# Expert weights through a ring of eight 2 MB slots in order of use, with loops over four experts, in a hybrid decoder block

## The chip, the cores and the metric

One Trainium2 chip, one core of it. The metric is the device time of one execution in microseconds; the kernel before was run three times and its median stands for it.

## What is computed

A decoder block for 512 tokens of width 1024, all in float32: RMS norm, an input projection, two attention mixers (NSA with compressed, selected and window keys; FoX with forget gates), gated output projections, a residual sum x2, and a mixture of 32 experts, four for each token. The part the change touches is the mixture:

```
logits = xt @ router_w + router_b;  top_v, top_i = top_k(logits, 4);  gate = softmax(top_v)
# for each expert e, over the tokens routed to it
hc  = xb @ w1[e] + b1[e]                      # (tokens, 1024) @ (1024, 2048)
gt  = minimum(hc[:, :1024], 7);  up = clip(hc[:, 1024:], -7, 7)
y   = ((up + 1) * gt * sigmoid(1.702 * gt)) @ w2[e] + b2[e]     # @ (1024, 1024)
out = x2 + sum of gate * y;  then a final RMS norm
```

An expert's weights are 8 MB (w1) and 4 MB (w2); all 32 have to be read once, 402 MB.

## The kernel before

The program is written engine by engine, with semaphores. The attention part takes the time to about 445 us, the output projection and the routing the time to about 536 us. PE then runs expert after expert: `expert(e, b, before)` (L1652) runs `up` (L1614), the product with w1 for 96 token slots in three groups of 32, and then `second(e - 1, ...)` (L1675) with `down` (L1628), the product with w2 for the expert before. `up` reads w1 in eight slabs of 1 MB, `down` reads w2 in four. Each matmul works on 32 columns of the array (`tile_position`), four beside each other. Expert 0 to 2 and 31 are written out; experts 3 to 30 stand in a hardware loop whose body has two of them (L1692):

```python
            with pe.Fori(0, (E - 4) // 2) as i:
                expert(2 * i + 3, 1, True)
                expert(2 * i + 4, 0, True)
```

The weights lie in `ring` (L162), twelve slabs of 1 MB, loaded in pairs of 2 MB by `load_pair` (L619) on the queue of SyncE (SP). The slots are tied to a place in an expert: pairs 0 to 3 hold w1, pairs 4 and 5 hold w2. SP waits until PE has used a pair (`w1_used`, `w2_used`) and loads the same pair of a later expert; the order of its loads is w1 of expert e + 1, then w2 of expert e (L667). Before the experts `ring` holds attention weights, so w1 of expert 0 is loaded as these come free, from 441 us on, and w2 of expert 0 behind the first gather.

Around the start of expert 0 SP also stores the normalized rows (`store_table`, L631) and the residual rows `xs` (`store_x2`, L635) to DRAM. The last table store must land before GpSimd (POOL) may gather expert 0's rows from the table (L831), PE turns them (`turned_x`), VectorE (DVE) scales them (L2158), and expert 0 begins. Routing: DVE writes one-hot rows in `qk` (`mark`, L2053); PE's `fill_table` makes the table of slots from them, and `fill_gates` (L1536), 33 small matmuls behind expert 0's `up`, the gates' part for the last tile, which DVE takes up in `take_gates` (L2084).

`up` writes PSUM banks 0 to 2 for every expert, the bias bank is 3, `down` writes 4 and 5. DVE reads banks 0 to 2 in `biased` (L2180) and then gives them back with `hc_free` (L2202); PE waits for it before the next `up` (L1657). ScalarE (ACT) copies the bias bank (`take_b_up`, L1140), takes the sigmoid, and scales `down`'s result by the gate (`take_y`); POOL adds it to x2 in DRAM by indirect DMA (`scattered`, L853).

Behind the experts every engine passes a loop for overflow blocks (L1701), whose body is jumped over when an expert has no more than 96 tokens; 21 rounds. Then x2 is read back, normalized with the gain `gf_b` and stored.

## Time and profile before

| | us |
|---|---|
| three runs | 1585.99, 1589.96, 1591.88 (median 1589.96) |
| profiled execution, its own time | 1584.68 |
| its span | 1582.9 |
| PE matmuls busy | 1534.0 (97%) |
| weight loads (PEld) busy | 849.8 (54%) |
| VectorE, GpSimd, ScalarE busy | 510.6, 312.5, 247.4 |
| granted PE clock, mean | 0.99 |
| DMA | 468 MB, 296 GB/s over the span |

The profile covers one execution. Each engine has a line of busy time; PE's weight loads overlap its matmuls. "PEq" or "PEldq" is PE's sequencer, which runs branches and register instructions, SPq is the queue of DMA issues. The chain of waits follows what released each step back from the last instruction.

### The profile page before, as it was taken

The numbers are of one execution on the slowest core, as the hardware profiler recorded it, in microseconds if no ns is written. First come the engines' busy times: TensorE is split into PE (matmuls) and PEld (weight loads), VectorE is DVE, ScalarE is ACT, GpSimd is POOL, SyncE is SP. The second block draws the span as 40 slices with busy tenths as digits, with TensorE's granted clock in tenths as the row PEclk, the third lists the DMA queues.
The fourth block names the chain that finished last, engine by engine and source line by source line (L and its number), as shares of the span: only waits on it lengthen the run. The fifth ranks groups of instructions, "written<-read, shape, count | busy, mean of one in ns | idle before, by whom it ended". The sixth has DMA issues, their size and how long they took to land.

```text
span 1582.9 us, 31267 instructions
## 1 busy us (share of the span) xinstructions
PE 1534.0 (97%) x13039; PEld 849.8 (54%) x13040; DVE 510.6 (32%) x941; ACT 247.4 (16%) x509; POOL 312.5 (20%) x449
## 2 busy tenths in 40 slices
PE   7999999999999999999999999999999999999993
PEld 4655555665445533566666666666664334555331
DVE  4104555242425542233223322332232223322232
ACT  4213443232422100000000000010001000000001
POOL 2000002342200202122212121222122212121101
PEclk9999999999999999999999999999999999999997
DMA  8121131521261599999999999999999999999986
GB/s 237 27 66 42 40 80 27 170 80 30 66 263 53 214 397 407 406 414 414 413 407 415 415 410 409 414 415 410 409 417 414 409 409 416 414 415 408 413 350 216
DMA packets 108446, 468.17 MB, mean 296 GB/s; under 512 B 29591, under 2 KB 71615, under 8 KB 83794
## 3 DMA queue, kind: packets, MB, share of 16 engines
q1 hardware_dynamic: 94610, 446.55, 70.1%
q0 software_dynamic: 13792, 21.00, 6.0%
q8 instruction: 31, 0.51, 0.1%
q14 instruction: 13, 0.11, 0.0%
HBM read 452.41 MB, written 19.29 MB: 298 GB/s over the span
## 4 chain that ended last, share of the span: by engine, by line
PE 78%; DMA 17%; DVE 2%; issue 1%; ACT 1%; SPq 0%; DVEq 0%; PEld 0%; POOL 0%; ACTq 0%; PEldq 0%; POOLq 0%
PE ps L1624 33%; DMA ring<-in_expert_w 16%; PE ps L1220 12%; PE ps L1642 10%; PE ps L1367 7%; PE ps L1646 5%; PE ps L1556 4%; PE ps L1352 2%; PE ps L1329 2%; PE ps L1339 1%; ACT mixT L1023 1%; DMA ring<-x 0%; DMA xs<-in_x 0%; PE ps L1508 0%; PE ps L1532 0%
## 5 line engine op out<-in xcount | busy, mean ns | idle before, releaser
L1624 PE MATMUL ps<-ring,oT_fox 128*32 128x512 f32 x6144 | 671.4, 592 | 2.8 <-DMA ring<-in_expert_w 2.8
L1624 PEld LDWEIGHTS ps<-ring,oT_fox 128*32 128x32 f32 x6144 | 333.5, 110 | 317.0 <-issue 278.9
L1642 PE MATMUL ps<-ring,hT 128*32 128x512 f32 x2048 | 292.7, 592 | 0.9 <-DMA ring<-in_expert_w 0.9
L2182 DVE TENSOR_TENSOR mixT<-ps,mask 128x768 f32<-128x768 f32 x64 | 61.0, 953 | 680.1 <-PE ps L1624 680.1
L1646 PE MATMUL ps<-ring,hT 128*32 128x256 f32 x2048 | 186.1, 379 | 0.0
L1646 PEld LDWEIGHTS ps<-ring,hT 128*32 128x32 f32 x2048 | 110.3, 110 | 106.1 <-issue 103.0
L1367 PE MATMUL ps<-hT,ring 128*128 128x512 f32 x304 | 137.0, 597 | 0.0
L1147 ACT ACTIVATE mixT<-mixT 128x768 f32<-128x768 f32 x32 | 27.0, 845 | 616.3 <-DVE mixT L2186 616.3
L1642 PEld LDWEIGHTS ps<-ring,hT 128*32 128x32 f32 x2048 | 100.3, 110 | 22.0 <-DMA ring<-in_expert_w 1.8
L843 POOL DMA_INDIRECT oT_nsa<-table,pc x93 | 100.6, 1082 | 47.4 <-POOL pc L838 28.0
L1220 PE MATMUL ps<-hT,ring 128*128 128x512 f32 x208 | 90.4, 593 | 0.2 <-ACT hT L953 0.2
L838 POOL COPY pc<-pc 128x3 int32 (+1 forms) x31 | 5.9, 191 | 427.3 <-DMA x<-hT,v_win 395.0
L1367 PEld LDWEIGHTS ps<-hT,ring 128*128 128x128 f32 x304 | 55.4, 190 | 63.7 <-issue 63.7
L1157 ACT ACTIVATE hT<-ps,v_fox 128x512 f32<-128x512 f32 x64 | 33.7, 577 | 270.3 <-PE ps L1646 270.3
L863 POOL COPY pT<-pT 96x32 bf16 (+1 forms) x64 | 15.4, 242 | 253.7 <-ACT hT L1157 239.8
L1220 PEld LDWEIGHTS ps<-hT,ring 128*128 128x128 f32 x208 | 39.1, 190 | 47.9 <-issue 47.7
L1023 ACT ACTIVATE mixT<-ps,st 128x128 f32<-128x128 f32 (+1 forms) x96 | 49.1, 536 | 78.8 <-DVE st L1855 78.8
L1556 PE MATMUL ps<-ring,mixT 128*128 128x512 f32 x128 | 59.0, 601 | 2.1 <-DVE qk L1986 2.1
L854 POOL DMA_INDIRECT x<-hT,v_win x32 | 52.1, 1629 | 39.4 <-POOL v_win L851 24.5
L2171 DVE STREAM_TRANSPOSE oT_fox<-oT_nsa 128x768 f32<-128x768 f32 x31 | 49.6, 1601 | 13.3 <-DVE mixT L2190 6.8
L856 POOL DMA_INDIRECT x<-hT,v_win x32 | 50.5, 1579 | 9.8 <-issue 9.8
L2178 DVE STREAM_TRANSPOSE hT<-mixT 128x768 f32<-128x768 f32 x32 | 51.3, 1604 | 1.1
(303 smaller groups left out, 1148.7 us busy)
## 6 DMA issues: line engine op xcount, KB each, us to landing
ring<-in_expert_w SPq DMA_DIRECT2D x192, 2048.0 KB
ring<-in_w_in SPq DMA_DIRECT2D x28, 512.0 KB, 5.0
ring<-in_w_out SPq DMA_DIRECT2D x8, 512.0 KB, 8.7
ring<-in_w_in SPq DMA_DIRECT2D x1, 2144.0 KB, 12.8
xs<-in_x SPq DMA_DIRECT2D x4, 512.0 KB, 5.2
ring<-in_w_in SPq DMA_DIRECT2D x8, 256.0 KB, 3.6
ring<-in_w_proj_nsa SPq DMA_DIRECT2D x16, 128.0 KB, 2.8
ring<-in_w_proj_fox SPq DMA_DIRECT2D x8, 256.0 KB, 3.2
```

The costliest lines, as they stand in the source:

```text
L843: pool.indirect_dma_start(out=xg_rows[b][:, 256 * g:256 * g + 256], out_offset=None, in_=table_quarter, in_offset=bass.IndirectOffsetOnAxi ...
L854: pool.indirect_dma_start(out=x2_half, out_offset=bass.IndirectOffsetOnAxis(ap=now_half[b], axis=0), in_=yb[b][:, 0:512], in_offset=None, ...
L856: pool.indirect_dma_start(out=x2_quarter, out_offset=bass.IndirectOffsetOnAxis(ap=now_quarter[b], axis=0), in_=yb[b][:, 512:768], in_offse ...
L1023: last = act.activation(probs[:, h, P_OFF[t]:P_OFF[t] + P * (t + 1)], scores(h, t), ACT.Exp, bias=ngm[:, h, t:t + 1], accum_out=sums[:, h, ...
L1220: last = pe.matmul(dst, lhs(c), rhs(c), start=(c == 0), stop=(c == n - 1))
L1367: ins = pe.matmul(w, w_c(c), hT[:, c, :], start=(c == 0), stop=(c == NK - 1))
L1556: ins = pe.matmul(ps[:, u, :], mixT[:, k, t * P:(t + 1) * P], w_o[k][:, n * 512:(n + 1) * 512], start=(k == 0), stop=(k == NK - 1))
L1624: ins = pe.matmul(wide(ps[TG * j:TG * j + TG, g, :]), xT[b][:, g, c, :], up_slab(c, j), start=(c == 0), stop=(c == NK - 1), tile_position= ...
L1642: pe.matmul(ps[TG * q:TG * q + TG, 4, :], gT[b][:, q // 2, c, :], ring[:, NK + j, at:at + 512], start=False, stop=(c == NK - 1), tile_posi ...
L1646: ins = pe.matmul(ps[TG * q:TG * q + TG, 5, 0:256], gT[b][:, 2, c, :], ring[:, NK + j, at:at + 256], start=False, stop=(c == NK - 1), tile ...
L2178: return dve.transpose(gT[b], act_b.rearrange("p g (m c) -> p g c m", c=NK))
L2182: return dve.tensor_tensor(to, half, b_up[:, 256 * n:256 * n + 256].unsqueeze(1).broadcast_to([P, NG, 256]), ALU.add)
```

## The change

Two more slots join the ring, so that it has eight of 2 MB. Slot 6 is `xs`, the residual rows, free when the last of them is stored. Slot 7 is a new tensor `x0` of 4096 columns, which holds what were `qk` (one-hot rows and attention queries), `rope_cos`, `rope_sin`, `pcT` and `cmp_one`; it is free when `fill_gates` has read the one-hot rows.

The loads go through the slots in the order in which PE uses them: w1 of expert 0, w1 of expert 1, w2 of expert 0, w1 of expert 2, w2 of expert 1, and so on, load number n into slot n mod 8, once load n - 8 has been used. Six loads an expert and eight slots come round after four experts, so the loops of SP and PE have bodies of four experts and seven passes instead of 14 for PE.

Expert 0's `up` writes banks 5 to 7 and the gates' late part bank 2, so that expert 1 need not wait for `hc_free`. `fill_gates` moves to behind the third slab of expert 0, `take_gates` on VectorE ahead of the rows of expert 1, and expert 1 waits for `rows_ready` at its start. ACT's copy of the bias of expert 1 now waits for `hc_free`. The final gain goes to `xs` only when all of w2 has been used.

```diff
+SLOTS = 8
...
-        qk = sb("qk", [P, 4, S])
+        x0 = sb("x0", [P, 4096])
+        qk = x0[:, 0:4 * S].rearrange("p (a s) -> p a s", a=4)
...
-        pcT = sb("pcT", [P, S])
+        pcT = x0[:, 6 * S:7 * S]
...
-        cmp_one = sb("cmp_one", [P, NT, 2, NCP])
-        rope_cos = sb("rope_cos", [P, S])
-        rope_sin = sb("rope_sin", [P, S])
+        cmp_one = x0[:, 7 * S:7 * S + NT * 2 * NCP].rearrange("p (t h c) -> p t h c", t=NT, h=2)
+        rope_cos, rope_sin = (x0[:, n * S:(n + 1) * S] for n in (4, 5))
...
-        hc_g, hc_u = ps[:, 0:NG, 0:256], ps[:, 0:NG, 256:512]
+        HC, HC_FIRST = 0, BANKS - NG
+        hc_g, hc_u = ([ps[:, at:at + NG, 256 * n:256 * n + 256] for at in (HC, HC_FIRST)] for n in range(2))
...
-            return ps[0:CAP, 5, 3 * e:3 * end].rearrange("p (e v) -> p e v", v=3)
+            return ps[0:CAP, 2, 3 * e:3 * end].rearrange("p (e v) -> p e v", v=3)
...
+        def pair_slot(k):
+            if k < 6:
+                return ring[:, 2 * k:2 * k + 2, :].rearrange("p c n -> p (c n)")
+            return xs_f if k == 6 else x0[:, :]
+        def slab(k, h):
+            return pair_slot(k)[:, 2048 * h:2048 * h + 2048]
+        def up_slab(k, h, j):
+            return slab(k, h).rearrange("p (n j m) -> p n j m", n=2, j=4)[:, :, j, :]
+        class Order:
+            def __init__(self, i, r):
+                self.i, self.r = i, r
+            def w1(self, u):
+                return Fill(self.i, 6 * self.r - 2 + u if self.r else u)
+            def w2(self, u):
+                return Fill(self.i, 6 * self.r + 8 + u if self.r < E - 1 else 6 * self.r + 4 + u)
+        class Fill:
+            def __init__(self, i, at):
+                self.slot, self.landed = at % SLOTS, 48 * i + 16 * (at // SLOTS + 1)
...
-            load_pair(0, 0)
+            load_w1_pair(0, 0, 0)
             sp.wait_ge(mix_sig, NK)
             for u in range(1, 3):
-                load_pair(0, u)
+                load_w1_pair(0, u, u)
             sp.wait_ge(mix_full, NK)
-            load_pair(0, 3)
+            load_w1_pair(0, 3, 3)
             for t in range(NT - 1):
                 store_x2(t)
                 store_table(t)
             sp.wait_ge(out_full, 2 * NT)
+            load_w1_pair(1, 0, 4)
             store_table(NT - 1)
             sp.wait_ge(xg_loaded[0], 16)
             store_x2(NT - 1)
-            for u in range(NK // 2, 6):
-                load_pair(0, u)
-            def load_w1(e):
-                for u in range(NK // 2):
-                    sp.wait_ge(w1_used, NK * (e - 1) + 2 * u + 2)
-                    load_pair(e, u)
-            def load_w2(e):
+            load_w1_pair(1, 1, 5)
+            sp.wait_ge(x2_stored, 16 * (NT + 1))
+            load_w1_pair(1, 2, 6)
+            sp.wait_ge(table_full, NT + 3)
+            load_w1_pair(1, 3, 7)
+            def load_w2(e, order):
                 for u in range(2):
-                    sp.wait_ge(w2_used, 4 * (e - 1) + 2 * u + 2)
-                    load_pair(e, NK // 2 + u)
-            load_w1(1)
-            with sp.Fori(1, E - 1) as e:
-                load_w1(e + 1)
-                load_w2(e)
-            load_w2(E - 1)
-            sp.wait_ge(x2_stored, 16 * (NT + 1))
+                    if order.r == E - 1:
+                        sp.wait_ge(w2_used, 4 * (e - 2) + 2 * u + 2)
+                    elif isinstance(e, int) and e == 0:
+                        sp.wait_ge(w1_used, 2 * u + 2)
+                    else:
+                        sp.wait_ge(w1_used, NK * e + 2 * (u + 2) + 2)
+                    load_w2_pair(e, u, order.w2(u).slot)
+            def load_w1(e, order):
+                for u in range(4):
+                    if u >= 2:
+                        sp.wait_ge(w1_used, NK * (e - 1) + 2 * (u - 2) + 2)
+                    elif isinstance(e, int) and e == 2:
+                        sp.wait_ge(w1_used, 2 * (u + 2) + 2)
+                    else:
+                        sp.wait_ge(w2_used, 4 * (e - 3) + 2 * u + 2)
+                    load_w1_pair(e, u, order.w1(u).slot)
+            load_w2(0, Order(0, 0))
+            load_w1(2, Order(0, 2))
+            load_w2(1, Order(0, 1))
+            with sp.Fori(0, (E - 4) // 4) as i:
+                for r in range(3, 7):
+                    load_w1(4 * i + r, Order(i, r))
+                    load_w2(4 * i + r - 1, Order(i, r - 1))
+            load_w1(E - 1, Order(0, E - 1))
+            load_w2(E - 2, Order(0, E - 2))
+            load_w2(E - 1, Order(0, E - 1))
+            sp.wait_ge(w2_used, 4 * E)
...
                 act.wait_ge(w1_used, NK * e + 1)
+                if isinstance(e, int) and e == 1:
+                    act.wait_ge(hc_free, 1)
                 act.activation(b_up, ps[:, NG, :], ACT.Copy).then_inc(b_up_ready, 1)
...
-            def expert(e, b, before):
+            def expert(e, b, before, order):
+                fills = [order.w1(u) for u in range(4)]
                 pe.wait_ge(xT_ready, e + 2)
-                if before:
+                if isinstance(e, int) and e == 1:
+                    pe.wait_ge(b_up_ready, 1)
+                    pe.wait_ge(rows_ready, 1)
+                elif before:
                     pe.wait_ge(hc_free, e)
                 pe.wait_ge(pick_up_ready, e + 1)
@@ -1660,19 +1716,28 @@
                     ins.then_inc(w1_used, 1)
                     if isinstance(e, int) and e == 0 and c == 0:
                         spread_slots()
+                    if isinstance(e, int) and e == 0 and c == 2:
+                        fill_gates()
                     if isinstance(e, int) and e == 1 and c == NK // 2:
-                        pe.wait_ge(rows_ready, 1)
                         spread_rows(4, 0, 2 * E, row_of.rearrange("p v e -> p (v e)")).then_inc(table_full, 1)
                 if not before:
                     pe.wait_ge(parts_taken, 1)
-                up(b, lambda c: pe.wait_ge(slabs_loaded[c // 2], 16 * e + 16) if c % 2 == 0 else None, used)
+                def loaded(c):
+                    if c % 2 == 0:
+                        pe.wait_ge(slabs_loaded[fills[c // 2].slot], fills[c // 2].landed)
+                up(b, [f.slot for f in fills], loaded, used, HC if before else HC_FIRST)
                 if before:
-                    second(e - 1, 1 - b)
-                else:
-                    fill_gates()
-            def second(e, b):
+                    second(e - 1, 1 - b, Order(order.i, order.r - 1))
...
             keep_clock(2)
-            expert(0, 0, False)
-            expert(1, 1, True)
-            expert(2, 0, True)
-            with pe.Fori(0, (E - 4) // 2) as i:
-                expert(2 * i + 3, 1, True)
-                expert(2 * i + 4, 0, True)
-            expert(E - 1, 1, True)
-            second(E - 1, 1)
+            for e in range(3):
+                expert(e, e % 2, e > 0, Order(0, e))
+            with pe.Fori(0, (E - 4) // 4) as i:
+                for r in range(3, 7):
+                    expert(4 * i + r, r % 2, True, Order(i, r))
+            expert(E - 1, 1, True, Order(0, E - 1))
+            second(E - 1, 1, Order(0, E - 1))
...
             count_extra()
+            take_gates()
             take_x(1, 1, gather)
             expert(0, 0, None)
-            take_gates()
             after_first()
             with dve.Fori(0, E // 2 - 1) as i:
```

`load_w1_pair` and `load_w2_pair` do what `load_pair` did, with the slot given; in `down` the operand `ring[:, NK + j, ...]` becomes `slab(slots[j // 2], j % 2)`.

Two places in the engines' order show the moves. SP, from the last residual and table stores to its expert loop; first before, then with the change (`x<-in_expert_w` is the slot in `x0`, `xs<-in_expert_w` the one in `xs`):

```order
L633 DMA table<-hT 128x1024 [waits x_normed]
L633 DMA table<-hT 128x1024 [waits x_normed,out_full]
L637 DMA x<-xs 128x1024 [waits x2_ready,xg_loaded0]
L628 DMA ring<-in_expert_w 128x4096 x2
L628 DMA ring<-in_expert_w 128x4096 [waits w1_used] x4
L667 UNCONDITIONAL_BRANCH
L667 ISA
```

```order
L664 DMA table<-hT 128x1024 [waits x_normed]
L654 DMA ring<-in_expert_w 128x4096 [waits out_full]
L664 DMA table<-hT 128x1024 [waits x_normed]
L668 DMA x<-xs 128x1024 [waits x2_ready,xg_loaded0]
L654 DMA ring<-in_expert_w 128x4096
L654 DMA xs<-in_expert_w 128x4096 [waits x2_stored]
L654 DMA x<-in_expert_w 128x4096 [waits table_full]
L660 DMA ring<-in_expert_w 128x4096 [waits w1_used] x2
L654 DMA ring<-in_expert_w 128x4096 [waits w1_used] x4
L660 DMA xs<-in_expert_w 128x4096 [waits w1_used]
L660 DMA x<-in_expert_w 128x4096 [waits w1_used]
L714 UNCONDITIONAL_BRANCH
L714 ISA
```

A load of expert 1 now stands ahead of the last table store and three behind the last residual store, where two loads of w2 of expert 0 stood. Those now follow the whole of expert 1's w1.

PE from the second half of expert 0's `up` to the first matmuls of expert 1; before, then with the change:

```order
L1624 MATMUL ps<-ring,oT_fox 32x512 [waits slabs_loaded2]
L1624 MATMUL ps<-ring,oT_fox 32x512 x23
L1624 MATMUL ps<-ring,oT_fox 32x512 [waits slabs_loaded3]
L1624 MATMUL ps<-ring,oT_fox 32x512 x23
L1538 MATMUL ps<-kT_win,qk 96x96 [waits gates_ready]
L1541 MATMUL ps<-v_sel,qk 96x3 x32
L1618 MATMUL ps<-pT 32x512 [waits pick_up_ready,hc_free,xT_ready]
```

```order
L1674 MATMUL ps<-ring,oT_fox 32x512 x11
L1588 MATMUL ps<-kT_win,x 96x96 [waits gates_ready]
L1591 MATMUL ps<-v_sel,x 96x3 x32
L1674 MATMUL ps<-ring,oT_fox 32x512 x12
L1674 MATMUL ps<-ring,oT_fox 32x512 [waits slabs_loaded2]
L1674 MATMUL ps<-ring,oT_fox 32x512 x23
L1674 MATMUL ps<-ring,oT_fox 32x512 [waits slabs_loaded3]
L1674 MATMUL ps<-ring,oT_fox 32x512 x23
L1668 MATMUL ps<-pT 32x512 [waits rows_ready,pick_up_ready,b_up_ready,xT_ready]
```

The two rows of the gate matmuls moved up into expert 0, and the first matmul of expert 1 waits for `b_up_ready` and `rows_ready` where it waited for `hc_free`.

## Rows read from the trace of the kernel before

**Rows 1.** The page: busy time of each engine, and busy tenths in 40 slices.

```profile
PE 1534.0 (97%) x13039; PEld 849.8 (54%) x13040; DVE 510.6 (32%) x941; ACT 247.4 (16%) x509; POOL 312.5 (20%) x449
...
DMA  8121131521261599999999999999999999999986
```

**Rows 2.** Stretches: us, busy (x) PE, PEld, DVE, ACT, POOL, PEclk, DMA share, GB/s.

```profile
656.20:750.60 94.40, 94.40 (x1001) 60.14 (x996) 26.83 (x27) 7.54 (x13) 21.69 (x30) 1.00 1.02 412
...
1405.60:1470.20 64.60, 64.13 (x676) 33.11 (x668) 17.90 (x19) 4.99 (x8) 15.33 (x21) 1.00 1.02 413
```

**Rows 3.** The chain of waits in order of time: start us, us, what.

```profile
593.15 20.60 PE ps L1624 x144
...
1191.22 20.79 PE ps L1624 x185
...
1212.17 26.50 DMA ring<-in_expert_w
...
1238.71 5.40 PE ps L1624 x48
...
1470.21 26.48 DMA ring<-in_expert_w
...
1512.96 20.60 PE ps L1624 x192
...
1543.78 0.48 PE ps L1646 x8
...
1557.13 0.48 PE ps L1646 x8
```

**Rows 4.** Timeline of PE: start us, us, engine, line; in expert 22, and at the end.

```profile
1222.65 15.63 PE L1624 MATMUL ps<-ring,oT_fox 128*32 128x512 f32 x144
...
1533.38 0.40 PE L1631 MATMUL ps<-pT 96*32 96x512 bf16 x4
...
1545.43 0.40 PE L1631 MATMUL ps<-pT 96*32 96x512 bf16 x4 [1.22 <-issue]
```

**Rows 5.** Timeline before the first gather; GB/s in 521 to 536 us; gather to landing.

```profile
520.37 1.10 PE L1556 MATMUL ps<-ring,mixT 128*128 128x512 f32 x2
...
526.15 0.32 SPq L633 DMA_DIRECT2D table<-hT  x1
...
534.91 12.99 SPq L628 DMA_DIRECT2D ring<-in_expert_w  x4
...
GB/s 0 0 0 0 0 0 0 0 0 0 0 0 0 0 0 76 382 404 437 98 0 0 0 0 0 0 0 0 44 98 98 251 273 109 22 0 0 0 317 393
...
DMA to landing us min/median/max: 4.7/4.7/4.7
```

**Rows 6.** Timeline, PE and VectorE where expert 1 begins.

```profile
557.73 0.24 PE L1538 MATMUL ps<-kT_win,qk 128*96 128x96 f16 x1
...
561.05 0.40 PE L1618 MATMUL ps<-pT 96*32 96x512 bf16 x4 [1.68 <-issue]
...
552.68 1.59 DVE L2171 STREAM_TRANSPOSE oT_fox<-oT_nsa 128x768 f32<-128x768 f32 x1 [6.44 <-DMA oT_nsa<-table,pc]
```

**Rows 7.** DMA in 593 to 691 us, then 700 to 1500: packets, MB, share.

```profile
DMA packets 3904, 40.05 MB, mean 409 GB/s; under 512 B 600, under 2 KB 988, under 8 KB 1584
...
q8 instruction: 8, 0.13, 0.5%
...
DMA packets 32483, 329.76 MB, mean 412 GB/s; under 512 B 5191, under 2 KB 8547, under 8 KB 13366
...
oT_nsa<-table,pc POOLq DMA_INDIRECT x75, 7.6
```

**Rows 8.** The branch of the expert loop, and the weight load behind it.

```profile
L1692 PEldq COMPARE_BRANCH  x14: 76/208/208, 685.6 to 1511.0; - x14
...
686.94 0.24 PEld L1618 LDWEIGHTS ps<-pT 96*32 96x32 bf16 x4
```

**Rows 9.** The branch over the overflow body: min/median/max ns.

```profile
L1702 PEldq COMPARE_BRANCH  x21: 214/214/3357, 1559.9 to 1578.1; - x21
```

More of the change, by code:

```diff
@@ L460, in hybrid_block @@
         idx_ready = sem("idx_ready")
-        slabs_loaded = [sem("slabs_loaded%d" % b) for b in range(6)]
+        slabs_loaded = [sem("slabs_loaded%d" % b) for b in range(SLOTS)]
         w1_used = sem("w1_used")
@@ L1612, in wide, with up @@
                 return c.rearrange("p (n m) -> p n m", n=2)
-            def up(b, loaded, used):
+            def up(b, slots, loaded, used, hc=HC):
                 for j in range(4):
@@ L1623, in up, with down @@
                         for j in range(4):
-                            ins = pe.matmul(wide(ps[TG * j:TG * j + TG, g, :]), xT[b][:, g, c, :], up_slab(c, j),
+                            ins = pe.matmul(wide(ps[TG * j:TG * j + TG, hc + g, :]), xT[b][:, g, c, :],
+                                            up_slab(slots[c // 2], c % 2, j),
                                             start=(c == 0), stop=(c == NK - 1), tile_position=(0, TG * j))
                     used(c, ins)
-            def down(b, loaded, used):
+            def down(b, slots, loaded, used):
                 for q in range(4):
@@ L1637, in down @@
                     j, h = c // 2, c % 2
+                    rows = slab(slots[j // 2], j % 2)
                     if h == 0:
@@ L1668, in expert, with second, loaded @@
                     pe.wait_ge(parts_taken, 1)
-                up(b, lambda c: pe.wait_ge(slabs_loaded[c // 2], 16 * e + 16) if c % 2 == 0 else None, used)
+                def loaded(c):
+                    if c % 2 == 0:
+                        pe.wait_ge(slabs_loaded[fills[c // 2].slot], fills[c // 2].landed)
+                up(b, [f.slot for f in fills], loaded, used, HC if before else HC_FIRST)
                 if before:
-                    second(e - 1, 1 - b)
-                else:
-                    fill_gates()
-            def second(e, b):
+                    second(e - 1, 1 - b, Order(order.i, order.r - 1))
+            def second(e, b, order):
+                fills = [order.w2(u) for u in range(2)]
+                def loaded(j):
+                    if j % 2 == 0:
+                        pe.wait_ge(slabs_loaded[fills[j // 2].slot], fills[j // 2].landed)
                 pe.wait_ge(gT_ready, e + 1)
@@ L1682, in second @@
                 pe.wait_ge(pick_down_ready, e + 1)
-                down(b, lambda s: pe.wait_ge(slabs_loaded[(NK + s) // 2], 16 * e + 16) if s % 2 == 0 else None,
-                     lambda s, ins: ins.then_inc(w2_used, 1))
+                down(b, [f.slot for f in fills], loaded, lambda j, ins: ins.then_inc(w2_used, 1))
             pe.wait_ge(count_taken, 1)
@@ L1716, in _ @@
                     pe.wait_ge(ov_w, 192 * o + 192)
[L1717 removed]
+                    up(0, range(4), lambda c: None, lambda c, ins: ins.then_inc(ov_pe, 1) if c == NK - 1 else None)
                     pe.wait_ge(ov_dve, 3 * o + 3)
[L1719 removed]
+                    down(0, (4, 5), lambda s: None, lambda s, ins: ins.then_inc(ov_pe, 1) if s == 3 else None)
                     pe.wait_ge(ov_act, 2 * o + 4)
@@ L2260, in _ @@
                     dve.wait_ge(b_up_ready, E + o + 1)
-                    for n, (to, half) in enumerate(((gt_b, hc_g), (up_b, hc_u))):
+                    for n, (to, half) in enumerate(((gt_b, hc_g[0]), (up_b, hc_u[0]))):
                         biased(to, half, n).then_inc(ov_part, 1)
```

31 lines of the change are left out of this document (14 added, 17 removed).

## The prediction

> **What bounds the kernel now.** I read the page first. TensorE (PE) is busy for 97% of the span and the DMA slices stand at 9 from the middle of the run on [rows 1]: from about 535 us, where the experts begin, two resources are both nearly full. The table of stretches shows how they share the time. In 656 to 751 us PE is busy for 94.40 of 94.40 us while DMA moves 412 GB/s; in 1406 to 1470 us DMA moves 413 GB/s, no more, and PE is short of work for about half a microsecond [rows 2]. So DMA runs at its own pace in both stretches, and PE is a little faster than it.
>
> The chain of waits gives both paces. From the up projection that starts at 593.15 to the one at 1191.22 there are 19 experts: 598.07 / 19 = 31.48 us each, PE alone. From 1212.17 to 1470.21 the chain is a weight load and one pair of slabs, eight times: 258.04 / 8 = 32.26 us for an expert's six loads, 5.38 us a load, DMA alone [rows 3]. The loads lose 0.78 us an expert against PE until their lead is gone, at 1238.66. What that costs: 1512.96 - 593.15 = 919.8 us for 29 experts, against 29 x 31.48 = 912.9, so 6.9 us. At the end the last expert's w2 pairs may be loaded only when expert 30 has used the two slots. PE starts that last down projection at 1545.43 and ends it at 1557.13 + 0.48 = 1557.6, which is 12.2 us; the one before it went from 1533.38 to 1544.26, 10.9 us. That is 1.3 us more. Both together, **8.2 us**, are all that waiting for weights costs [rows 3, 4].
>
> **The change, part by part.** I follow PE's end, 1557.6 us in this trace. What comes behind it (gates, scatter-add, final norm, store) takes the last 25.3 us of the span of 1582.9 and stays. The norm's gain is now loaded only behind PE's last use of w2; it is needed in the final norm, when the scatter-add has landed and x2 has been read back, so I put it at nothing; without that cover it would be a 0.5 MB transfer, 1.3 us at 412 GB/s.
>
> (a) *Table store before the first gather.* One 2 MB load is now issued when the last output matmul is done, at about 521.5, before the table store of 526.15. The store's bytes move from 526.9 to about 528.3, and the gather waits for them [rows 5]. The load's bytes need 5.1 us at 412 GB/s from about 0.8 us behind its issue, so until 527.4: the store begins some 0.5 us later. I take **+0.5 us** (0 to +1.5) for the start of the first expert.
>
> (b) *First boundary.* Today PE runs the 33 small gate matmuls at 557.73 and then stands for 1.68 us, because expert 1 writes the same PSUM banks and waits until VectorE has read expert 0's [rows 6]. With other banks this wait goes; the gate matmuls merely move into expert 0. Late next would be expert 1's rows: VectorE transposes them at 552.68 for 1.6 us [rows 6] and scales them in about one; the gate work moved ahead of that, five small operations behind gate matmuls that end at about 547, fits into the 6.44 us that it stood for the gather. PE wants the rows at 559.5. So **-1.6 us** (-1.7 to 0).
>
> (c) *Order and number of slots.* The queue of loads starts again at 534.9 in both kernels, but four loads are behind it today and five in the new one; the seventh and the eighth slot are filled at about 538 and 547, while the queue is busy, so they add no gap. Every load thus lands one load earlier in the order of use, 5.4 us. In order of use the last w2 pairs wait for expert 29's slots and not for expert 30's. How far this reaches: w1 pair 3 of expert 22 lands at 1238.66; moved by 5.4 us it lands at 1233.3, where PE, which wants it at 1222.65 + 3 x 5.15 = 1238.1 today [rows 4] and 1.1 us earlier by (a) and (b), wants it at 1237.0: a lead of 3.7 us. It shrinks by 9 x 0.78 = 7.0 us until expert 31, which would wait 3.3 us. If PE is late for another reason by more than that, all 8.2 us of weight waits go: **-8.2 us** then, -4.9 us otherwise.
>
> (d) *The loop over four experts.* PE executes 1001 + 996 matmuls and weight loads in three experts [rows 2], 666 an expert: the loop's body grows from some 1,330 to some 2,660 instructions. In 593 to 691 us, with the first pass of the present loop, the instruction queue brings 8 packets, 0.13 MB; in 700 to 1500 us there is no row of it at all [rows 7]. So the present body stays with the engine once fetched (8 packets for 98 / 31.48 x 666 = 2,070 instructions, one per 259), and its backward branch takes 208 ns, hidden: it is executed 1.4 us before PE needs the next expert's first weights [rows 8]. What a branch costs whose target is not held stands in one row: the first jump over the overflow body, about one expert's instructions ahead, took 3357 ns, the 20 behind it 214 [rows 9]. Will the new body still be held? The only far jump in the trace paid at about 700 instructions, and blocks arrive just ahead of need, none in advance; I take it that a body twice as long is not held, and that each of the six backward branches (seven passes) pays that way. That is a choice: no row shows a backward jump over more than 1,330 instructions.
>
> The Trainium skill, "Runtime: NRT & Kernel Launch", section "Instruction fetch mechanics", says that PE has 128 KiB for 2,048 instructions, refilled in blocks of 256 as a FIFO, and that a taken branch to something outside its window must fetch first. By that rule the new body does not fit. The trace agrees with the block (259 by the rows) and with the stall (3.36 us); the same page's two-block window is at odds with a body of five blocks that runs without a fetch, so for that the trace decides.
>
> The price on PE's path: the branch starts at 685.6; 3.36 us later it ends at 688.9, 0.45 us of register instructions follow, and the first weights go in at 689.4 where today it is 686.94: 2.4 us. That row was taken with DMA nearly idle. Under full load a gather takes 7.6 us to land against 4.7 when idle [rows 5, 7], 1.6 times: 3.15 x 1.6 = 5.1 us instead of 3.15, so 4.4 us on PE's path. The low end, with the register instructions hidden as well, is 2.0. I take **3.3 us**, in the middle, since the load is full but an instruction packet is one piece of 16 KB and a gather is many: 6 x 3.3 = **+19.8 us** (+12 to +26.4). PE never waits for anything else in the loop, so nothing absorbs it; the loads only gain more lead by it.
>
> The sum: +0.5 - 1.6 - 8.2 + 19.8 = **+10.5 us**. The profiled execution took 1584.68 us, so 1595.2 by it; the median of the three runs is 1589.96, 5.3 us above, so **1600.5 us** against that median.
>
> **The rivals.** *Rival 1: the longer body is held* (or a backward branch is foreseen). For it: 1,330 instructions are held today and nothing shows the limit. Against it: the 3357 ns row. Then PE is tied to the loads again from about expert 27 on: 0.5 - 1.6 - 4.9 = -6.0 us, 1584.0 us, between -9.3 (loads a little faster, no wait left) and -3. The point that decides: the branch must cost PE less than (8.2 + 1.1) / 6 = 1.6 us, a little less with the 3.3 us wait counted; then the kernel is faster.
>
> *Rival 2: the instruction packets slow the weights.* If the body is fetched anew in every pass, 8 packets in 98 us are 0.5% of 16 engines, 0.98 us a packet [rows 7]. On one engine alone that is 2.6 us an expert, and as a load lands only when its slowest engine is done, 28 experts would run at up to 34.9 us instead of 32.26: the stream would end 73 us later, and the time be near 1657 us. Against it: in just that stretch DMA moved 409 GB/s against 412 without the packets [rows 7] and the experts stayed at PE's 31.5 us. I give it little.
>
> **How the numbers follow.** A measurement of this kernel tells about 0.5%, 8 us, from no change. Forecast (all six branches pay): 0.70; its own range is +2.7 to +17, 1592 to 1607, with up to 3 us more if a second block is late behind the first. Of it 0.48 lies over +8 us, 0.22 within. Rival 1: 0.25, of which 0.09 beyond -8 and 0.16 within. Rival 2: 0.03, slower. Left over 0.02, half slower, half faster. Slower 0.52, same 0.38, faster 0.10. The range of 8 in 10 takes in most of rival 1 and the costly end of the branches: 1581 to 1610.
>
> **What would show it.** The new loop's COMPARE_BRANCH on PE's sequencer: seven, six of them over 3 us where the old took 0.21, each followed by a pause on PE of 2 to 4.5 us, every fourth expert and 126 to 130 us apart. Instruction packets (16 KB) in the middle of the run, some 2.6 an expert. No wait for in_expert_w on PE anywhere behind expert 2. The pause of 1.68 us at the first boundary gone. The first gather up to 1 us later. A branch of 0.2 us with the instruction queue silent would make the prediction wrong, and rival 1 right; a branch of 3.4 us or more with experts further apart than 31.5 us between the branches would speak for rival 2.

## The result, and the profile after

The changed kernel takes **1625.63 us** (median of 6 runs, 1623.51 to 1626.20), the kernel before on the same chip 1590.48: a ratio of **1.0224, interval 1.0207 to 1.0241**. That is 35 us slower, where the prediction had 10.5 us and a range up to 1610. The profiled execution took 1625.79 us, its span is 1624.0, so 41.1 us more than the span of before. (The profiled execution of before, 1584.68, lies nearly 6 us under its median, so the spans differ by more than the medians.)

The page of the changed kernel, its busy times, the granted clock, the instruction queue and the chain that ended last:

```profile
PE 1543.3 (95%) x13039; PEld 645.7 (40%) x13040; DVE 511.4 (31%) x941; ACT 247.6 (15%) x509; POOL 317.8 (20%) x449
...
DMA  8121130611342899999999999999999999999954
...
q8 instruction: 114, 1.87, 0.5%
...
PE 92%; issue 3%; DVE 1%; ACT 1%; DMA 1%; SPq 0%; DVEq 0%; PEld 0%; POOL 0%; PEldq 0%; POOLq 0%; ACTq 0%
```

Against [rows 1] the matmuls are as many and PE is busy for 9.3 us more with them, in a span 41 us longer. The instruction queue carries 114 packets, where before it had 31. DMA, which held 15.6% of the chain of before by its waits for weights alone, has 1% left; in its place stands "issue".

All that PE waited for from expert 1 to the last, in the view of waits (engine, line, releaser: us in total, times, longest):

```profile
PE ps L1668 <- issue: 32.6, 6, 5.7
PE ps L1682 <- issue: 1.2, 1, 1.2
```

No weight is waited for any more; six waits for "issue" stand ahead of L1668, the first matmul of an expert. What PE's sequencer did there, as in [rows 8], and the jump over the overflow body, as in [rows 9] (min/median/max ns):

```profile
L1755 PEldq COMPARE_BRANCH  x7: 76/6913/7124, 749.0 to 1549.6; - x7
...
L1765 PEldq COMPARE_BRANCH  x21: 214/214/3727, 1597.2 to 1615.9; - x21
```

The seventh branch leaves the loop and takes 76 ns. The six that go back take 6.6 to 7.1 us, where before they took 0.21 and where the prediction had 3.36. One of them in the timeline of PE (start us, us, line, operation, idle time ahead), and the table of stretches around it (us, busy (x) PE, PEld, DVE, ACT, POOL, PEclk, DMA share, GB/s):

```profile
750.21 0.64 PE L1698 MATMUL ps<-x,hT 128*32 128x256 f32 x8
756.52 0.62 PE L1668 MATMUL ps<-pT 96*32 96x512 bf16 x4 [5.67 <-issue]
```

```profile
749.00:751.00 2.00, 1.85 (x28) 0.70 (x20) 0.67 (x1) 0.00 (x0) 0.00 (x0) 1.00 1.04 422
751.00:753.00 2.00, 0.00 (x0) 0.00 (x0) 0.00 (x0) 1.05 (x2) 0.45 (x3) 1.00 1.04 418
753.00:755.00 2.00, 0.00 (x0) 0.00 (x0) 0.00 (x0) 0.00 (x0) 1.51 (x1) 0.94 0.97 393
755.00:757.00 2.00, 0.47 (x8) 0.34 (x12) 0.00 (x0) 0.00 (x0) 1.69 (x2) 0.50 1.04 442
757.00:759.00 2.00, 2.00 (x16) 0.49 (x12) 0.00 (x0) 0.00 (x0) 0.02 (x1) 0.50 1.00 402
759.00:761.00 2.00, 2.00 (x12) 0.38 (x8) 0.00 (x0) 0.00 (x0) 0.00 (x0) 0.50 1.01 360
761.00:763.00 2.00, 2.00 (x20) 0.54 (x16) 0.00 (x0) 0.60 (x1) 0.00 (x0) 0.85 1.03 369
763.00:765.00 2.00, 2.00 (x24) 0.58 (x20) 0.00 (x0) 0.00 (x0) 0.00 (x0) 1.00 1.05 405
```

So a branch costs twice. PE stands for 5.67 us, and towards the end of that the granted clock falls to 0.50, that is from 2.4 to 1.2 GHz, and stays there while PE is already at work: in 757 to 761 it does 28 matmuls, in 763 to 765 24 in half the time. The experts' start times give the price. From 719.2 to 756.5 to 790.5 two experts take 37.3 and 34.0 us, against 31.47 where PE sets the pace: 5.8 us of standing and 2.5 us of slow clock. All six branches add up to 33.8 us of the one and 11.5 of the other. Over the whole loop, from 593.3 to 1551.2, 29 experts take 957.9 us; at the prediction's pace they would take 29 x 31.48 = 912.9, which is **45.0 us, or 7.5 a branch** (45.3 by the starts of this trace, 31.47 each).

The start, and the end, have one surprise each. The timeline before the first gather, as in [rows 5]:

```profile
521.62 0.33 SPq L654 DMA_DIRECT2D ring<-in_expert_w  x1
...
526.22 0.32 SPq L664 DMA_DIRECT2D table<-hT  x1
...
528.82 0.15 DVE L2124 TENSOR_SCALAR v_win<-ps 96x1 int32<-96x1 f32 x1 [0.28 <-PE ps L1582]
...
531.03 1.25 POOL L879 DMA_INDIRECT oT_nsa<-table,v_win  x1 [6.65 <-DMA table<-hT]
```

The indices are ready at 528.97 and the gather is issued 2.06 us later, released by the table store, behind the early load's bytes. Before it was 0.9 us, released by the indices:

```profile
529.79 1.46 POOL L831 DMA_INDIRECT oT_nsa<-table,v_win  x1 [5.53 <-DVE v_win L2061]
```

The first expert starts at 537.7 instead of 536.4. PE has little to do in this gap, and the granted clock then reads 0.50 for 3.4 us, into the first matmuls of expert 0; before it stayed at 1.00. SP's queue behind PE's last matmul, at 1594.9, and the same rows before:

```profile
1594.97 0.33 SPq L723 DMA_DIRECT2D xs<-in_norm_f_g  x1
1606.68 1.76 SPq L743 DMA_DIRECT2D ring<-x  x4
```

```profile
1544.66 0.43 SPq L674 DMA_DIRECT2D xs<-in_norm_f_g  x1
1565.55 1.76 SPq L695 DMA_DIRECT2D ring<-x  x4
```

x2 is read back 11.8 us behind PE's end; before, with PE's end at 1557.6 and the gain's load issued 13 us ahead of it, x2 was read back 7.9 us behind. The slow clock at the start and the later read at the end are not in the prediction.

The first boundary, which stands in [rows 6] for before:

```profile
547.13 0.24 PE L1588 MATMUL ps<-kT_win,x 128*96 128x96 f16 x1
547.21 1.56 PE L1591 MATMUL ps<-v_sel,x 128*96 128x3 f16 x32
548.70 13.08 PE L1674 MATMUL ps<-ring,oT_fox 128*32 128x512 f32 x120
561.60 0.40 PE L1668 MATMUL ps<-pT 96*32 96x512 bf16 x4
```

The gate matmuls lie inside expert 0 and the pause of 1.68 us is gone.

### The profile page after: what moved, and what is told of

Read it like the earlier page. It is cut to its first block, busy times and chain, and to the rows that moved or that the text cites. A ratio compares the mean times of both kernels' runs of the same rounds, so it can differ in the third digit from the quotient of the medians.

```text
span 1624.0 us, 31137 instructions
## 1 busy us (share of the span) xinstructions
PE 1543.3 (95%) x13039; PEld 645.7 (40%) x13040; DVE 511.4 (31%) x941; ACT 247.6 (15%) x509; POOL 317.8 (20%) x449
## 4 chain that ended last, share of the span: by engine, by line
PE 92%; issue 3%; DVE 1%; ACT 1%; DMA 1%; SPq 0%; DVEq 0%; PEld 0%; POOL 0%; PEldq 0%; POOLq 0%; ACTq 0%
PE ps L1674 41%; PE ps L1694 14%; PE ps L1270 12%; PE ps L1698 7%; PE ps L1417 7%; PE ps L1606 3%; PE ps L1402 2%; PE ps L1379 2%; PE ps L1389 1%; ACT mixT L1071 1%; PE ps L1668 1%; PE ps L1682 0%; DMA ring<-x 0%; PE ps L1558 0%; PE ps L1279 0%
## 5 line engine op out<-in xcount | busy, mean ns | idle before, releaser
L1674 PE MATMUL ps<-ring,oT_fox 128*32 128x512 f32 x4704 | 522.3, 603 | 0.0
L1674 PEld LDWEIGHTS ps<-ring,oT_fox 128*32 128x32 f32 x4704 | 155.0, 112 | 349.4 <-issue 345.6
L1694 PE MATMUL ps<-ring,hT 128*32 128x512 f32 x1472 | 191.5, 592 | 0.0
L1698 PE MATMUL ps<-ring,hT 128*32 128x256 f32 x1472 | 113.0, 379 | 0.0
L1698 PEld LDWEIGHTS ps<-ring,hT 128*32 128x32 f32 x1472 | 47.8, 110 | 110.0 <-issue 109.9
L1674 PE MATMUL ps<-xs,oT_fox 128*32 128x512 f32 x720 | 80.2, 592 | 0.0
L1674 PE MATMUL ps<-x,oT_fox 128*32 128x512 f32 x720 | 80.0, 592 | 0.0
L911 POOL COPY pT<-pT 96x32 bf16 (+1 forms) x64 | 20.9, 328 | 285.5 <-ACT hT L1207 271.0
L1606 PE MATMUL ps<-ring,mixT 128*128 128x512 f32 x128 | 59.0, 601 | 2.1 <-DVE x L2049 2.1
L1694 PEld LDWEIGHTS ps<-ring,hT 128*32 128x32 f32 x1472 | 47.3, 110 | 30.2
```

The lines of the kernel that those rows point to most:

```text
L1606: ins = pe.matmul(ps[:, u, :], mixT[:, k, t * P:(t + 1) * P], w_o[k][:, n * 512:(n + 1) * 512], start=(k == 0), stop=(k == NK - 1))
L1674: ins = pe.matmul(wide(ps[TG * j:TG * j + TG, hc + g, :]), xT[b][:, g, c, :], up_slab(slots[c // 2], c % 2, j), start=(c == 0), stop=(c == ...
L1694: pe.matmul(ps[TG * q:TG * q + TG, 4, :], gT[b][:, q // 2, c, :], rows[:, at:at + 512], start=False, stop=(c == NK - 1), tile_position=(0, ...
L1698: ins = pe.matmul(ps[TG * q:TG * q + TG, 5, 0:256], gT[b][:, 2, c, :], rows[:, at:at + 256], start=False, stop=(c == NK - 1), tile_positio ...
```

## The experiments

Three theories stood after the result. A: the branches of the longer loop body cost it all. B: instruction packets slow the weights, now or as soon as PE is not held up. C: the new ring, its order or its early load cost something of their own. (Theory 1 of the first expectations is A, theory 2 is C.)

**PE's loop written out, in both kernels.** First in the changed kernel:

```diff
-            with pe.Fori(0, (E - 4) // 4) as i:
-                for r in range(3, 7):
-                    expert(4 * i + r, r % 2, True, Order(i, r))
+            for e in range(3, E - 1):
+                expert(e, e % 2, True, Order(0, e))
```

> The changed kernel with PE's 28 looped experts written out; slots, order, banks and SP's loop stay. Theory 1 (the six backward branches over a body that PE no longer holds cost everything: 7.5 us each, 5.7 of standing and 1.8 of halved clock, 45 us in all): no branch over 1 us and no clock of 0.50 between 545 and 1500 us, experts 31.5 us apart, a wait for weights of about 3 us near expert 31, time 1583 to 1586 us, ratio to the kernel before 0.995 to 0.998. Theory 2 (the eight-slot order or the new slots in xs and x0 hold PE up): the pauses of 5.7 us stay at every fourth expert, time above 1610 us.

Measured: 1593.79 us, ratio 1.0036 (1.0022 to 1.0049). The kernel before took 1587.17 us beside it, so 6.6 us are left of the 35: some 28.5 us went with the branches. Theory A holds for the bulk, but the time is 8 us over the upper end of its expectation. PE waits for weights again, 12 times and 9.3 us in all (waits of PE in the whole expert part):

```profile
PE ps L1674 <- DMA ring<-in_expert_w: 6.3, 8, 1.8
...
PE ps L1674 <- DMA x<-in_expert_w: 1.1, 2, 0.6
PE ps L1694 <- DMA xs<-in_expert_w: 1.0, 1, 1.0
PE ps L1674 <- DMA xs<-in_expert_w: 0.9, 1, 0.9
```

They begin near expert 20, and from the expert at 1193.3 to the one at 1487.0 nine take 32.63 us each, where the kernel before has 32.26. The queue of instructions has 65 packets in 700 to 1500. Another 3.1 us of the miss lie behind PE's end, 28.4 us where before has 25.3; what they are is shown under "The end". The same edit in the kernel before:

```diff
-            with pe.Fori(0, (E - 4) // 2) as i:
-                expert(2 * i + 3, 1, True)
-                expert(2 * i + 4, 0, True)
+            for e in range(3, E - 1):
+                expert(e, e % 2, True)
```

> The kernel before with PE's loop written out, nothing else. Theory 1: its body of 1,341 instructions is held and its branch hidden, so 1589 to 1592 us, ratio 0.999 to 1.001, with instruction packets all through the run. Rival (a hardware loop costs PE something even when its body is held, or the packets of a written-out program slow the weights): over 2 us away from the kernel before.

Measured: 1598.74 us, ratio 1.0069 (1.0051 to 1.0086). Here only PE's loop, and with it the way its instructions come, differs from before. From 1037.3 to 1492.8 fourteen experts take 32.54 us each, and the waits set the pace some six experts earlier than in [rows 3]. **Fetching 2.6 packets of 16 KB an expert costs the stream of weights 0.3 to 0.4 us an expert**, 1%. The three kernels with PE's loop written out pay it (32.54, 32.63 and, with the early load in halves, 32.62 us), the short loops do not (32.26 before, 32.2 in both kernels of "What can be had without the ring"). Theory B is right in kind, at an eighth of what rival 2 had. Not all of the loss here is packets: of the 14.5 us by which the profiled span is longer, 1.6 lie ahead of the first expert, and 1.6 are a clock of 0.50 behind the pause at the first boundary, which did not fall in the trace of before. In the changed kernel the packets cost nothing, since PE is late by more.

**The loop body alone.** The kernel before, with its six slots, and four experts in PE's body:

```diff
-            with pe.Fori(0, (E - 4) // 2) as i:
-                expert(2 * i + 3, 1, True)
-                expert(2 * i + 4, 0, True)
+            with pe.Fori(0, (E - 4) // 4) as i:
+                for r in range(3, 7):
+                    expert(4 * i + r, r % 2, True)
```

> The kernel before with PE's loop body of four experts instead of two, six slots and order as before. Theory 1: six backward branches of 6.5 to 7.1 us, the clock at 0.50 behind each, 6 x 7.5 = 45 us more, of which 8 us are given back because PE no longer waits for weights: 1625 to 1630 us. Theory 2: 1590 us.

Measured: 1624.98 us, ratio 1.0237 (1.0219 to 1.0254), the changed kernel's within the interval. Its branch:

```profile
L1692 PEldq COMPARE_BRANCH  x7: 76/6961/7147, 747.5 to 1548.0; - x7
```

The loss is in the body of the loop and not in the ring. From expert 2 to expert 31 this kernel takes 957.8 us, the changed one 957.9, and it too waits for no weight in the loop.

**Does the load make the fetch slow?** The changed kernel, with 64 of the 4096 columns of each slot loaded for the experts of SP's loop (it leaves out most of these experts' weights, so it does not compute the block):

```diff
+                few = 4096 if isinstance(e, int) else 64
...
-                sp.dma_start(pair_slot(k), src.rearrange("e p n -> (e p) n")).then_inc(slabs_loaded[k], 16)
+                sp.dma_start(pair_slot(k)[:, 0:few], src.rearrange("e p n -> (e p) n")).then_inc(slabs_loaded[k], 16)
```

> The changed kernel, but SP's loop loads 64 columns of each slot instead of 4096, so DMA is nearly idle under the expert loop (most weights of experts 3 to 30 are not loaded; all waits stay). It asks what made the branch 6.6 to 7.1 us. Theory 1a (the fetch stands behind the weight packets on the DMA engines): the six backward branches take 3.3 to 3.8 us, like the forward jump at the end of every kernel here, PE stands 2 to 2.5 us at each, the clock falls less often or not. Theory 1b (a backward branch to code not held costs 7 us by itself, for instance because two blocks must come): they stay at 6.5 us or more.

Measured, in a single run: 1603.59 us, and

```profile
L1757 PEldq COMPARE_BRANCH  x7: 76/4164/4313, 747.9 to 1527.3; - x7
...
752.46 0.40 PE L1670 MATMUL ps<-pT 96*32 96x512 bf16 x4 [2.74 <-issue]
```

The branch takes 3.8 to 4.3 us with DMA at 31 GB/s and 6.6 to 7.1 with it at 402: the load adds 2.7 us. That is a factor of 1.66 (6.91 against 4.16 us). The price at light load is over what was expected from the jump behind the experts (3.3 to 3.9 us in the runs). Whether that is the direction or the kind of the branch, or the small loads and gathers that remain, is open.

**Where the limit lies.** The body of before is 1,341 instructions for a pass, matmuls, weight loads and sequencer's own together; that of the change 2,675. Writing the up matmuls of one, two or all three groups as two of half width makes bodies of 1,565, 1,789 and 2,013, with two experts as before and the same sums:

```diff
-                            ins = pe.matmul(wide(ps[TG * j:TG * j + TG, g, :]), xT[b][:, g, c, :], up_slab(c, j),
-                                            start=(c == 0), stop=(c == NK - 1), tile_position=(0, TG * j))
+                            to = wide(ps[TG * j:TG * j + TG, g, :])
+                            for n in (range(2) if more and c and g in (0, 1) else (slice(0, 2),)):
+                                ins = pe.matmul(to[:, n, :], xT[b][:, g, c, :], up_slab(c, j)[:, n, :],
+                                                start=(c == 0), stop=(c == NK - 1 and n != 0), tile_position=(0, TG * j))
```

> The kernel before with two experts in PE's loop body, in which the up matmuls of two groups are each written as two of half the columns: 1,789 instructions in the body instead of 1,341. If PE holds 2,048 as the notes say and the window slides by blocks of 256, this body is still held: branches of 0.2 us, no instruction packets between 700 and 1500 us. If less is held, branches of some 7 us. The time rises in any case with the added matmuls.

> As r6 with all three groups cut: 2,013 instructions in the body, under 2,048 by 35. Held (0.2 us branches, no packets in the loop) if all of 2,048 serve; not held (branches of some 7 us and a packet for every 256 instructions) if one block or two of the store are taken by fetching ahead. I expect not held.

> The kernel before with the up matmuls of one of the three groups (expert c = 1's share of the body, first group) written as pairs of half width, so that a pass of the PE's loop is 1,565 instructions; the same products and sums. A body of 1,341 had only a short branch at its end and one of 1,789 had 13 branches of 6.0 to 6.5 us. Theory A (the limit lies near the middle of the page's 2,048 less the blocks in flight): 1,565 is held, no branch above 0.3 us, about 31 instruction packets. Theory B (whatever is clearly over 1,341 is fetched anew): 13 branches of 6 us again and about 140 packets, 80 us more than without them.

Measured, in a single run each: 1682.86 (1,789), 1680.17 (2,013) and 1584.84 us (1,565). The branch of the body of 1,789, and of that of 1,565:

```profile
L1694 PEldq COMPARE_BRANCH  x14: 79/6305/6522, 689.8 to 1606.2; - x14
```

```profile
L1694 PEldq COMPARE_BRANCH  x14: 76/207/208, 685.2 to 1510.8; - x14
```

The bodies of 2,013 and of 1,789 are fetched anew, 13 times at about 7.5 us; both speak against the theory that all 2,048 instructions which the Trainium skill gives ("Runtime: NRT & Kernel Launch", section "Instruction fetch mechanics") can serve a loop. 1,565 is held: 32 packets in the whole run, where before has 31, and 31.50 us an expert, so the added matmuls are not what costs the other two their 95 us. So **the limit for a loop of PE lies between 1,565 and 1,789 instructions** in this kernel. Packets came one per 259 instructions in [rows 7], so in blocks of about 256, and seven of these are 1,792. That a body must touch fewer than eight blocks would fit, but no run shows it: sizes between 1,565 and 1,789 were not tried, nor the same size at another place in the program.

**The start.** The written-out form of the changed kernel with its early load in halves, 1 MB ahead of the last table store and 1 MB behind it:

```diff
-            load_w1_pair(1, 0, 4)
+            sp.dma_start(pair_slot(4)[:, 0:2048], ...[1, :, 0, 0:2048]).then_inc(half_loaded, 16)
             store_table(NT - 1)
+            sp.dma_start(pair_slot(4)[:, 2048:4096], ...[1, :, 0, 2048:4096]).then_inc(slabs_loaded[4], 16)
```

> As r1, and the 2 MB load that stands ahead of the last table store is cut in two: 1 MB ahead of the store, 1 MB behind it. Theory 1 with (a) of the prediction: expert 0 starts at 536.4 to 536.7 instead of 537.7, the clock of 0.50 at 536.3 goes, so 1.3 + 0.8 = 2 us of PE's time come back; as the weight stream is the bound near the end and starts about 1 us earlier too, 1 to 2 us faster than r1. Rival (the late start is not from the load's bytes but from the gather itself): start stays at 537.7, same time as r1.

Measured: 1592.29 us, ratio 1.003 (1.002 to 1.004), 1.5 us under the same form with the whole load; the two intervals overlap, so the traces have to tell. The first expert starts 1.0 us earlier and the first boundary is 1.0 us shorter, since the clock no longer falls. And the changed kernel with the load behind the first gather:

```diff
-            load_w1_pair(1, 0, 4)
             store_table(NT - 1)
             sp.wait_ge(xg_loaded[0], 16)
+            load_w1_pair(1, 0, 4)
```

> The changed kernel with its early 2 MB load of expert 1's weights moved behind the last table store and the first gather. If the load ahead of the store is what makes the first expert late: the first up matmul near 536.5 us instead of 537.7, no half clock at 536.3, and 1.2 + 0.8 = 2 us less than the changed kernel, about 1623.5 us, ratio to before 1.021. The six branches stay at 6.6 to 7.1 us. Rival: another wait takes its place (expert 1's weights late by one load), and the time is the changed kernel's within 0.5 us.

Measured: 1622.67 us, ratio 1.0216 (1.0198 to 1.0233), again within the changed kernel's interval. The first expert starts at 537.5, but everything up to the output projection was 0.9 us later in this execution; counted from the last matmul of that projection (L1606), it is 16.1 us instead of 17.2, and before 16.1. The clock in 537 to 539:

```profile
537.00:539.00 2.00, 1.80 (x19) 0.61 (x21) 1.76 (x9) 0.00 (x0) 0.00 (x0) 1.00 0.76 319
```

1.00, where the changed kernel has 0.50. From the first expert to the second it takes 22.9 us; before 24.6, changed 23.9. So the early load cost 1.1 us of delay, and the new banks are worth 1.7 us when the clock holds. The 1 us of clock is not certain to come with the load: of four traces with the whole load ahead of the store the clock fell in three, and stayed at 1.00 in that of the next experiment.

**The end.** SP's wait for w2 and the gain's load moved from ahead of its overflow loop to behind it:

```diff
-            sp.wait_ge(w2_used, 4 * E)
-            sp.dma_start(gf_b, norm_f_g.unsqueeze(0).partition_broadcast(P)).then_inc(pos_loaded, 16)
             sp.wait_ge(extra_ready, 1)
...
                     e = sp.value_load(extra[0:1, bass.ds(o, 1)], min_val=0, max_val=E - 1)
+                    sp.wait_ge(w2_used, 4 * E)
...
+            sp.wait_ge(w2_used, 4 * E)
+            sp.dma_start(gf_b, norm_f_g.unsqueeze(0).partition_broadcast(P)).then_inc(pos_loaded, 16)
             for b in range(2):
```

> The changed kernel with SP's wait for all of w2 and the load of the final gain moved from ahead of SP's loop for overflow blocks to behind it (an overflow block, which does not occur here, gets a wait of its own). In the trace of the changed kernel SP issues the gain at 1594.97, then passes 21 rounds of that loop at 0.5 us each, and reads x2 back at 1606.68, 11.8 us behind PE's end; before it was 7.9 us. If these rounds are what makes the end 3.8 us longer: x2 read back again 7.9 to 8.3 us behind PE's end, span behind PE's end 25.3 to 25.7 us instead of 29.1, and 3.4 to 3.8 us less than the changed kernel, about 1622, ratio to before 1.020. The six branches stay. Rival: the scatter-adds (2 of 1.6 us on POOL) or the tables of ACT are late as well, and less than 1 us is won.

Measured: 1621.27 us, ratio 1.0197 (1.018 to 1.0214). SP's rows behind PE's end, now at 1593.56:

```profile
1593.62 0.34 SPq L740 DMA_DIRECT2D xs<-in_norm_f_g  x1
1601.65 1.75 SPq L744 DMA_DIRECT2D ring<-x  x4
```

8.1 us instead of 11.8, and 25.6 us from PE's end to the end of the span instead of 29.1. Shown by these rows (the intervals of the two times still touch): with the gain's wait ahead of it, the loop of 21 rounds, which SP used to pass while PE still worked, stood between PE's end and the last read.

**What can be had without the ring.** The kernel before, six slots and two experts a pass, with the parts that proved good: the other banks for expert 0, the gate matmuls inside it, `take_gates` ahead, and w2 pair 0 of expert 0 loaded half ahead of and half behind the last table store.

```diff
+            sp.dma_start(into[:, 0:2048], early[:, 0:2048]).then_inc(half_loaded, 16)
             store_table(NT - 1)
+            sp.dma_start(into[:, 2048:4096], early[:, 2048:4096]).then_inc(slabs_loaded[4], 16)
...
-                if before:
+                if isinstance(e, int) and e == 1:
+                    pe.wait_ge(b_up_ready, 1)
+                    pe.wait_ge(rows_ready, 1)
+                elif before:
                     pe.wait_ge(hc_free, e)
```

> The kernel before with its six slots and its loop over two experts, and only the parts of the change that need no longer loop: other PSUM banks for expert 0, the gate matmuls inside it, and one load ahead of the first gather (w2 pair 0 of expert 0, 1 MB before the table store, 1 MB behind it). Theory: the weight stream gets 5.4 us of lead, so 5 of the 8.2 us of waiting for weights go, and the pause of 1.7 us at the first boundary goes; the table store is a little late, +0.2 us: 5 to 7 us faster than the kernel before, ratio 0.9955 to 0.997. Rival (what is won at the first boundary is lost again to the weights, as DMA sets the end): 3 to 5 us faster, with longer waits for weights.

Measured: 1584.01 us, before 1587.51, ratio 0.9979 (0.997 to 0.9989): 3.5 us quicker, less than the 5 to 7 expected and within what its rival had, that the weights take back what the start wins. The second expert follows the first after 22.9 us, and the chain is PE alone for one more expert than in [rows 3]; behind that PE still waits for weights ten times. Then the last w2 goes into slots that come free early: pairs 0 and 1, as soon as the last up projection has used them.

```diff
-            load_w2(E - 1)
+            for u in range(2):
+                sp.wait_ge(w1_used, NK * (E - 1) + 2 * u + 2)
+                src = expert_w2[0].rearrange("e (p u c) n -> e p u (c n)", p=P, c=4)[E - 1, :, u, :]
+                sp.dma_start(ring[:, 2 * u:2 * u + 2, :].rearrange("p c n -> p (c n)"), src).then_inc(slabs_loaded[u], 16)
...
```

> The kernel of r8 (six slots, loop over two experts, other PSUM banks for the first expert) with the last expert's down weights loaded into the first two slots that its own up projection leaves, instead of those that expert 30's down projection leaves. Where the stream of weights sets the end (last ten experts), the last loads start earlier: 1 to 1.5 us less than r8, ratio to before 0.9965 to 0.9975. Rival: the slots of expert 31's first pairs come free no earlier than those of expert 30's last, and the time is r8's, ratio 0.998.

Measured: 1582.65 us, before 1589.07, ratio **0.996 (0.9947 to 0.9974)**, the lowest here, though its interval overlaps that of the kernel without this edit. SP issues the last load, and then the gain, long before the end:

```profile
1517.87 5.49 SPq L678 DMA_DIRECT2D ring<-in_expert_w  x2
1523.40 0.43 SPq L682 DMA_DIRECT2D xs<-in_norm_f_g  x1
```

where without this edit the last load was issued at 1542.79. From the start of the last up projection to PE's end it is 43.7 us instead of 45.1. Both gains are under 0.5%.

## Why the prediction was right and wrong

The balance of the two profiled spans, by the experts' start times and PE's end, against the steps of the prediction:

| step | forecast, us | measured, us |
|---|---|---|
| (a) table store, start of expert 0 | +0.5 | +1.3 |
| (b) first boundary | -1.6 | -0.7 |
| expert 1 | 0 | 0.0 |
| (c) waits for weights | -8.2 | -8.2 |
| (d) six branches | +19.8 | +45.0 |
| gain's load, behind PE's end | 0 | +3.8 |
| sum | +10.5 | +41.2 (spans: 41.1) |

**(d) had the right mechanism and the wrong size, and it makes 25 of the 31 us that were missing.** The place, the number of branches and their distance are as forecast, and the body alone, put into the kernel before, gives the whole loss. Two things were mis-sized. First, the branch takes 6.9 us and not 3.36, the time of one forward jump with DMA nearly idle. A backward branch takes 4.2 us even at 31 GB/s, and the full load stretches that by 1.66. The gather's factor of 1.6 was thus about right, but it was applied to too small a time, and the 4.4 us on PE's path that it gave were then taken as 3.3. Measured on the path are 5.6 us, over the upper bound. Second, no step asked what PE's standing does to its clock: 1.9 us more a branch. Rival 1, the longer body is held, fell. The rule of the Trainium skill ("Runtime: NRT & Kernel Launch", section "Instruction fetch mechanics") was on the right side for this body, as 2,675 are more than its 2,048; the trace of before could not show that the usable part is smaller.

**(c) was right to the tenth** (6.9 us in the loop, 1.3 at its end), in the case "PE late for another reason". But the 6.9 us are not the ring's work: six slots with the loop over four experts wait for no weight in the loop either. PE, made 45 us late, lets the weights get ahead with any order. What the ring itself gives here is the end: from the start of the last up projection to PE's end it is 43.7 us with it, 46.4 with six slots and the same loop. With PE's loop written out, where PE is not late, the changed kernel is 5.0 us faster than the one with six slots (1593.79 against 1598.74), its new banks included and in spite of its longer end.

**The cost of the gain's load was the step that failed outright.** "I put it at nothing" looked at the transfer and at who needs it, and not at what is queued behind the waiting instruction on SP: 21 rounds of half a microsecond and the read of x2. That accounts for 3.8 us, and the run with the wait behind the loop brought them back.

**(a)** was within its bounds as a delay, though over the 0.5 us taken; the slow clock behind it was not thought of and took more than half of **(b)**, which is -1.7 us where the clock holds.

**Rival 2** was right that packets take from the stream of weights, and wrong in the price, 0.3 to 0.4 us an expert instead of up to 2.6. In the changed kernel it hides; with PE's loop written out it and the longer end keep the ring's gain from showing. Such a kernel with the early load in halves and the gain's wait moved was not run; 1592.3 less the 3.8 us is an estimate of 1588.5, where the kernel before took 1587.2 beside it.

## What to carry to other kernels

Unrolling a loop further to make a pattern of slots come round has a price that stands in no instruction: count the instructions of a pass for the busiest engine, and if the next size is over what the trace shows as held (here over 1,565), look for a pattern that fits the present body, or expect microseconds for each backward branch, more under a full DMA load. A stop of the matmul engine can cost more than its length, since it can come back at half the clock; so sum standing and slow clock. When a wait is added to a queue, list everything that the queue does behind it up to the end of the kernel, loops with empty rounds too.

## What the runs showed of the hardware

- A backward branch of PE to instructions no longer held: 6.5 to 7.2 us in the loops over four experts at some 400 GB/s of DMA traffic, 5.9 to 6.7 us in the bodies of 1,789 and 2,013 at 377 to 379 GB/s, 3.8 to 4.3 us at 31 GB/s. The same branch to a held body: 0.21 us, and covered.
- Held: 1,341 and 1,565 instructions. Not held: 1,789, 2,013, 2,675.
- A stop of PE of 5.2 to 5.7 us brought the granted clock to 0.50 in all six cases of the changed kernel, for 6.8 us in four and for 3.4 us in two, before PE started again or within 0.2 us of it. The stops of 2.4 to 2.9 us with small loads still did it in four of six passes, at 1.6 to 1.7 us for the next expert, and the pause of 1.7 us at the first boundary in three of the six traces that have it, though not in that of the kernel before.
- 16 KB instruction packets every 12 us lengthened an expert's six loads from 32.26 to 32.5 to 32.6 us, though the mean rate reads 411 against 412 GB/s: the start times of the experts show it, the rate hardly.
